# A two-layer decoder step on one core: prompt attention with half-array matmuls, a fused bias and minimum, division on GpSimd and transposes in one pass

## The chip, the core and the metric

The program runs on one core of a Trainium2 chip. A core has five engines that work side by side and signal each other by semaphores: TensorE (PE; its weight loads are shown as PEld), VectorE (DVE), ScalarE (ACT), GpSimd (POOL) and SyncE (SP), which here only issues transfers. The metric is the device time of one execution in microseconds (us), lower is better. All arithmetic is float32.

## The reference

Two layers are computed, for a prompt of 512 tokens and for 8 sampling sequences of one token each. In each layer three token mixers run on one joint input projection: a gated recurrence, gated linear attention, and sparse attention. The change lies in the third, in its part for the prompt. There are 16 heads of width 64 in 4 groups of 4 heads; a group shares keys and values. For each query three attentions are taken and added with gates:

```python
s = jnp.einsum('bqgpd,bngd->bgpqn', q, kc)
dist = (q_pos[:, None] - c_end[None, :])
p_cmp = masked_softmax(s - sl * dist, c_end[None, :] <= q_pos[:, None])   # compressed keys, 32 of them
...
p = masked_softmax(s - sl * dist, dist >= 0)                              # selected blocks
...
p = masked_softmax(s - sl * dist, mask)                                   # window of 512
...
return gates[..., 0:1] * o_cmp + gates[..., 1:2] * o_slc + gates[..., 2:3] * o_win
```

`sl` is a slope that each head has of its own. With 512 prompt tokens the second and the third see all earlier keys, so both are full causal attentions, each with keys and values of its own.

## The kernel before

The kernel is written by hand in blocks. Each block gives every engine a list of instructions, semaphores order them across engines, and a block ends when all engines have ended their lists. A layer is a chain of such blocks; the one that is changed, "the stage" below, is the prompt attention, once in each layer. The block in front of it projects and normalizes keys, values and queries (`KTR`, `VR`, `NQ`), and the one behind it is the attention of the samples, which begins by loading cache pages.

The stage walks over `NT` = 4 tiles of 128 queries (i = 0 to 3), and the keys that tile i sees are n = 128, 256, 384 or 512. Per tile it walks over the 4 groups g, and per group over 9 units: one for the compressed keys (all four heads together, 32 keys each) and 8 with one head each, 4 of the second attention and 4 of the third. That makes 144 units in each layer, 128 of them with a head. For a unit with a head:

- `scores` (L1737) on TensorE: queries by keys into a PSUM bank. A head is only 64 wide, but the query tile holds a head of an even group in its upper 64 rows and one of an odd group in its lower 64. `KTR` therefore holds zeros in the rows that belong to the other group, and the matmul takes all 128 rows.
- `biased` (L1850) on VectorE adds minus slope times distance on the way from PSUM to a buffer `SC`; `maximum` (L1863) takes the negated maximum of a row.
- `exps` (L1797) on ScalarE: exponential with the sum of each row, which takes an ACTIVATE and an ACTIVATION_READ_ACCUMULATOR.
- `scale` (L1881) and `diagonal` (L1889) on VectorE: reciprocal of the sum, and a 128x128 diagonal matrix of that reciprocal times the gate.
- `turn` (L1756) on TensorE: the probabilities are turned and divided at once by a matmul with this diagonal. A float32 matmul is two records in the trace, a transpose (L1752, L1356) is one.
- `copy` (L1810) on ScalarE brings the turned probabilities from PSUM to `PT`.
- `values` (L1773): values by probabilities, once for each group and attention, over 512 columns (four heads). Its result has 64 rows, so it uses 64 of the array's 128 columns: upper or lower half by the parity of g.

The order on each engine is written out: the score of unit u+4, the bias of u+3, the maximum of u+2 and the exponential of u are issued around the turn of u, and `values` comes three units behind. GpSimd has no work in the stage. In the block ahead of it, it sets the zeros of `KTR` (L1534).

## Time and profile before

| | us |
|---|---|
| median of 3 runs (lowest, highest) | 4429.02 (4428.1, 4430.91) |
| profiled execution, span from first to last instruction | 4429.1 |
| PE busy | 4083.6 |
| PEld busy | 3151.3 |
| DVE busy | 1352.0 |
| ACT busy | 829.6 |
| POOL busy | 140.1 |

The profiled execution agrees with the median to 0.1 us, so the span needs no correction. A busy PE is not a PE at its peak: matmuls overlap, and the busy time counts the time from a first start to a last end. How fast TensorE works is read from how far starts stand apart.

### The profile page before, as it was taken

To read this page: it belongs to the slowest core of one execution; us is meant where nothing else is said; L and a number is where in the kernel's file an instruction comes from. 1 tells how busy PE (TensorE), PEld (TensorE's weight loads), DVE (VectorE), ACT (ScalarE), POOL (GpSimd) and SP (SyncE) were. 2 spreads that over 40 slices of the span, in tenths; PEclk is the share of its full clock that TensorE was granted. 3 is DMA by queue.
4 is the path that set the end of the run, shared out by engine and by line. 5 is a ranking of instruction groups with operands and counts; after the bars stand their busy time and mean duration, and the time that the engine had idled before them with its cause. 6 is when DMAs were issued, how large, how long until landed. Compare 5 with 4: busy or idle time off the path is not lost. (4 is left out here: it accounts for less than half of the span.)

```text
span 4429.1 us, 47158 instructions
## 1 busy us (share of the span) xinstructions
PE 4083.6 (92%) x18666; PEld 3151.3 (71%) x18666; DVE 1352.0 (31%) x3077; ACT 829.6 (19%) x1710; POOL 140.1 (3%) x148
## 2 busy tenths in 40 slices
PE   7998898899899999999988988988999999999999
PEld 5757654655688887888877576546557888888888
DVE  5516433576320001000064173336763200010001
ACT  2213131254210000000032231313542000000000
POOL 0000020000110000000000000200001100000000
PEclk9999898999899999999999998988998999999999
DMA  3110442210252122212122104512004422212121
GB/s 125 60 57 25 144 152 55 79 48 1 81 176 63 56 72 76 76 67 77 38 89 78 40 23 144 171 49 105 10 1 123 134 76 76 72 42 76 67 82 52
DMA packets 222171, 336.95 MB, mean 76 GB/s; under 512 B 56614, under 2 KB 122386, under 8 KB 217210
## 3 DMA queue, kind: packets, MB, share of 16 engines
q1 hardware_dynamic: 204474, 281.90, 19.6%
q0 software_dynamic: 8064, 43.00, 2.9%
q10 hardware_dynamic: 9408, 8.98, 0.6%
q8 instruction: 150, 2.46, 0.2%
q14 instruction: 75, 0.61, 0.0%
HBM read 313.49 MB, written 37.10 MB: 79 GB/s over the span
## 5 line engine op out<-in xcount | busy, mean ns | idle before, releaser
L360 PE MATMUL pair<-hT,ring 128*128 128x260 f32 (+1 forms) x6464 | 1464.1, 388 | 75.4 <-issue 39.1
L360 PEld LDWEIGHTS pair<-hT,ring 128*128 128x128 f32 (+1 forms) x6464 | 1236.9, 192 | 288.9 <-issue 86.3
L370 PE MATMUL pair<-ring,hT 128*128 128x512 f32 (+3 forms) x960 | 385.6, 567 | 30.5 <-PEq L1263 25.6
L370 PEld LDWEIGHTS pair<-ring,hT 128*128 128x128 f32 (+1 forms) x960 | 167.0, 194 | 237.6 <-issue 237.3
L2360 PE MATMUL pair<-arena,ring 128*128 128x260 f32 x1408 | 309.1, 383 | 1.8 <-DVE arena L2386 1.8
L2360 PEld LDWEIGHTS pair<-arena,ring 128*128 128x128 f32 x1408 | 267.4, 190 | 43.5 <-DVE arena L2386 2.5
L1756 PEld LDWEIGHTS pair<-arena 128*128 128x128 f32 x1280 | 170.8, 192 | 98.6 <-DVE arena L1889 74.9
L2325 DVE TENSOR_TENSOR arena<-pair,arena 128x520 f32<-128x520 f32 x48 | 33.6, 700 | 659.4 <-PE pair L360 659.4
L1756 PE MATMUL pair<-arena 128*128 128x128 f32 x1280 | 199.1, 287 | 22.4 <-DVE arena L1889 21.6
L2386 DVE TENSOR_TENSOR arena<-pair,arena 128x520 f32<-128x520 f32 x44 | 30.8, 700 | 601.3 <-PE pair L360 601.3
L1737 PE MATMUL pair<-arena 128*128 128x128 f32 (+3 forms) x512 | 192.2, 461 | 0.0
L1850 DVE SCALAR_TENSOR_TENSOR arena<-con,pair 128x128 f32<-128x128 f32 (+3 forms) x256 | 123.6, 483 | 167.5 <-PE pair L1737 164.6
L1371 PE MATMUL pair<-arena 128*128 128x512 f32 (+1 forms) x320 | 155.4, 571 | 10.3 <-DVE arena L1485 10.3
L797 PE MATMUL pair<-hT,ring 128*128 128x260 f32 x512 | 137.2, 415 | 25.9 <-DVE ocT L1052 25.9
L1810 ACT ACTIVATE ring<-pair 128x128 f32<-128x128 f32 (+3 forms) x256 | 111.7, 436 | 254.3 <-PE pair L1756 253.1
L2310 ACT ACTIVATE arena<-pair 128x520 f32<-128x520 f32 x48 | 28.9, 603 | 668.3 <-PE pair L360 668.3
L1773 PE MATMUL pair<-ring,arena 128*64 128x512 f32 x320 | 151.0, 602 | 1.4 <-ACT ring L1810 1.4
L1797 ACT ACTIVATE arena<-arena 128x128 f32<-128x128 f32 (+3 forms) x256 | 142.5, 557 | 13.7 <-DVE arena L1863 10.9
L2375 ACT ACTIVATE arena<-pair 128x520 f32<-128x520 f32 x44 | 26.5, 603 | 606.6 <-PE pair L360 606.6
L1737 PEld LDWEIGHTS pair<-arena 128*128 128x128 f32 x512 | 79.8, 198 | 75.6 <-issue 63.7
L797 PEld LDWEIGHTS pair<-hT,ring 128*128 128x128 f32 x512 | 101.6, 208 | 44.1 <-issue 29.7
L1356 PEld LDWEIGHTS pair<-con,arena 128*128 128x128 f32 (+1 forms) x640 | 78.7, 150 | 75.8 <-issue 73.2
(351 smaller groups left out, 4414.9 us busy)
## 6 DMA issues: line engine op xcount, KB each, us to landing
ring<-in_w_in_dram SPq DMA_DIRECT2D x38, 2048.0 KB, 9.2
ring<-in_w_ffn_gate_dram SPq DMA_DIRECT2D x10, 2048.0 KB, 7.8
ring<-in_w_ffn_up_dram SPq DMA_DIRECT2D x10, 2048.0 KB, 8.1
ring<-in_w_ffn_down_dram SPq DMA_DIRECT2D x8, 2048.0 KB, 7.7
out_s_win_kv_dram<-in_cache_win_kv_dram SPq DMA_DIRECT2D x2, 8176.0 KB
arena<-in_cache_slc_kv_dram SPq DMA_DIRECT2D x86, 128.0 KB
ring<-in_cache_slc_kv_dram SPq DMA_DIRECT2D x86, 128.0 KB
arena<-in_state_gla_dram SPq DMA_DIRECT2D x16, 512.0 KB
```

Source lines behind the costliest of these rows:

```text
L360: last = pe.matmul(pair[o][0:m, half, 0:HA], lhs(k), rhs[:, k, half * HA:(half + 1) * HA], start=(k == 0), stop=(k == nk - 1))
L370: last = pe.matmul(big[0:rows, 0:w], hT[:, k, tt * P:tt * P + rows], slab[:, k, 0:w], start=(k == 0), stop=(k == KT - 1))
L797: last = pe.matmul(pair[proj_pair(key)][:, half, 0:HA], gr[0][:, k, m % 4 * P:(m % 4 + 1) * P], hT[:, k, half * HA:(half + 1) * HA], start ...
L1356: last = pe.transpose(bank[4 + kv][:, g * P:g * P + n], R2[z // 2 % 3][0:n, kv * G + g, :], ident[0:n, 0:n])
L1371: pe.matmul(dst, PH[:, kv, 2 * qt + sp2_, :], src, start=(qt == 0 and sp2_ == 0), stop=(qt == 3 and sp2_ == 1)).then_inc(sem("ct_mm"), 1)
L1737: last = pe.matmul(out[:, 0:n], NQ[:, gp * 4 + p_, i * P:(i + 1) * P], KTR[br - 1][:, g, 0:n], start=True, stop=True)
L1756: last = pe.matmul(out[:, kt * P:(kt + 1) * P], SC[u % NSC][:, kt * P:(kt + 1) * P], DG[u % 4], start=True, stop=True)
L1773: last = pe.matmul(out, VR[br - 1][:, kt, g * DH:(g + 1) * DH], PT[br][:, kt, :], start=False, stop=(br == 2 and kt == i))
L1797: act.activation(s[:, 0:n], s[:, 0:n], ACT.Exp, bias=stat[:, u % NSC, 0, 0:1], accum_out=stat[:, u % NSC, 1, 0:1]).then_inc(sem("sa_e"), 1)
L1810: act.activation(PT[br][:, 0:i + 1, p_ * P:(p_ + 1) * P], src[:, 0:(i + 1) * P].rearrange("p (k t) -> p k t", t=P), ACT.Copy).then_inc(sem ...
L1850: dve.scalar_tensor_tensor(s[:, 0:n], dist[:, 384 - i * P:384 - i * P + n], -SLOPE[4 * g + p_], src[:, 0:n], ALU.mult, ALU.add).then_inc(s ...
L2360: last = pe.matmul(pair[m][:, half, 0:HA], w[:, k, m * P:(m + 1) * P], FA[:, r + k, half * HA:(half + 1) * HA], start=(r + k == 0), stop=( ...
```

## The change

A unit now takes two groups at once, an even one (a = 0) and an odd one (a = 1), so there are 72 units in each layer, 64 of them with two heads, and the work of a unit is that of two before.

- Keys are stored without zeros. The score of a head takes 64 rows of the array, upper or lower, and the two heads of a unit follow each other in different halves, into the two banks of a PSUM pair.
- The slope is moved: the queries are divided by minus the slope when they are normalized (`qsl`), and one VectorE instruction with an accumulator (`tensor_tensor_reduce`) adds the distance, multiplies by the slope and takes the minimum of each row. It is two instructions in the program, both shown as ISA. The exponential reads the result with scale -1.
- GpSimd multiplies the probabilities in `SC` by reciprocal and gate. The diagonal matrix goes, and `turn` is now a transpose.
- `values` runs for two heads of both groups (256 columns), the two groups in turn in different column halves.
- VectorE does one of the four copies of each two units, ScalarE the other three. Of `SC` there are 5 buffers for two heads instead of 7 for one.
- The zeros of `KTR` and `KCP` are no longer set.

```diff
-                        last = pe.matmul(out[:, 0:n], NQ[:, gp * 4 + p_, i * P:(i + 1) * P],
-                                         KTR[br - 1][:, g, 0:n], start=True, stop=True)
+                        for a in range(2):
+                            hf = slice(a * DH, (a + 1) * DH)
+                            q_ = NQ[hf, gp * 4 + h + p_, i * P:(i + 1) * P]
...
+                                last = pe.matmul(out[:, a, 0:n], q_, KTR[br - 1][hf, gp, 0:n], start=True, stop=True)
...
-                            last = pe.matmul(out[:, kt * P:(kt + 1) * P], SC[u % NSC][:, kt * P:(kt + 1) * P],
-                                             DG[u % 4], start=True, stop=True)
+                            last = pe.transpose(out[:, kt * P:(kt + 1) * P], SC[v % NSC][:, a, kt * P:(kt + 1) * P], ident)
...
-                            last = pe.matmul(out, VR[br - 1][:, kt, g * DH:(g + 1) * DH], PT[br][:, kt, :],
-                                             start=False, stop=(br == 2 and kt == i))
+                    for kt in range(1 if br == 0 else i + 1):
+                        for a in range(2):
...
+                                last = pe.matmul(out[:, (p_ - 1) * P:(p_ + 1) * P], VR[br - 1][:, kt, g * DH:(g + 1) * DH],
+                                                 PT[pt_slot(v)][:, a, kt, :], start=False, stop=(kt == i),
+                                                 skip_group_check=True)
...
+                for v in range(-AHEAD_S, NU + LAG_V):
+                    if v + AHEAD_S < NU:
+                        scores(v + AHEAD_S)
+                    if 0 <= v < NU:
+                        turn(v, 0)
+                        turn(v, 1)
+                    if v >= LAG_V and (units[v - LAG_V][2] == 0 or units[v - LAG_V][3] % 2):
+                        values(v - LAG_V)
...
+            @block.gpsimd
+            def _(pool):
...
+                    pool.wait_ge(sem("sa_r"), v + 1)
...
+                            pool.tensor_scalar(s[:, a, 0:n], s[:, a, 0:n], st[:, 1, a:a + 1], GATE[:, i, k:k + 1],
+                                               ALU.mult, ALU.mult).then_inc(sem("sa_p"), 1)
...
-                        dve.scalar_tensor_tensor(s[:, 0:n], dist[:, 384 - i * P:384 - i * P + n], -SLOPE[4 * g + p_],
-                                                 src[:, 0:n], ALU.mult, ALU.add).then_inc(sem("sa_read"), 1)
+                    for a in range(2):
+                        last = dve.tensor_tensor_reduce(s[:, a, 0:n], dist[:, 384 - i * P:384 - i * P + n], src[:, a, 0:n],
+                                                        SLOPE[4 * (2 * gp + a) + p_], 3e38, ALU.add, ALU.min,
+                                                        st[:, 0, a:a + 1])
...
+                for v in range(-AHEAD_B, NU):
+                    if v + AHEAD_B < NU:
+                        biased(v + AHEAD_B)
+                    if 0 <= v + AHEAD_R < NU:
+                        inverse(v + AHEAD_R)
+                    if v >= 0 and dve_copies(v):
+                        copy(v)
```

On TensorE, at the last query tile (512 keys), the order of before is this; a row is an instruction of the program with its line, result and operands, and "x4" says how often it follows itself:

```order
L1737 MATMUL pair<-arena 128x512
L1756 MATMUL pair<-arena 128x128 x4
L1737 MATMUL pair<-arena 128x512
L1756 MATMUL pair<-arena 128x128 x4
L1773 MATMUL pair<-ring,arena 64x512 x4
L1737 MATMUL pair<-arena 128x512
```

The order now, at the same place, where L1743 is the score, L1758 the transpose and L1777 the values:

```order
L1743 MATMUL pair<-arena 128x512 x2
L1758 MATMUL pair<-con,arena 128x128 x8
L1743 MATMUL pair<-arena 128x512 x2
L1758 MATMUL pair<-con,arena 128x128 x8
L1777 MATMUL pair<-ring,arena 64x256 x8
L1743 MATMUL pair<-arena 128x512 x2
```

Two scores now stand together, eight turns (two halves of four) follow, and values come after every second unit, that is after four heads' worth of scores, with eight matmuls of 256 columns.

On VectorE, at the last query tile, the order of before for one unit of one head and the start of the next:

```order
L1850 SCALAR_TENSOR_TENSOR arena<-con,pair 128x512
L1863 TENSOR_REDUCE arena<-arena 128x1
L1889 TENSOR_SCALAR arena<-con,arena 128x128
L1881 RECIPROCAL arena<-arena 128x1
L1850 SCALAR_TENSOR_TENSOR arena<-con,pair 128x512
```

Now, for one unit of two heads and the first of the next (the order repeats with that copy after every second unit):

```order
L1889 ISA arena<-con,pair 128x512
L1889 ISA arena 128x1
L1889 ISA arena<-con,pair 128x512
L1889 ISA arena 128x1
L1908 RECIPROCAL arena<-arena 128x2
L1915 COPY ring<-pair 128x4x128
L1889 ISA arena<-con,pair 128x512
L1889 ISA arena 128x1
```

The maximum has gone into the biased operation and the diagonal is gone; one reciprocal serves two heads, and the copy from PSUM is new on this engine.

## Rows read from the trace of the kernel before

**Rows 1.** The page: span, busy time of engines (share of the span) and instructions.

```profile
span 4429.1 us, 47158 instructions
PE 4083.6 (92%) x18666; PEld 3151.3 (71%) x18666; DVE 1352.0 (31%) x3077; ACT 829.6 (19%) x1710; POOL 140.1 (3%) x148
```

**Rows 2.** Windows over the stage in the first layer; PEclk is the granted clock.

```profile
core 0: us, PE busy (x) PEld busy (x) DVE busy (x) ACT busy (x) POOL busy (x), PEclk, DMA share, GB/s
869.00:900.00 31.00, 26.66 (x129) 18.39 (x130) 23.24 (x113) 17.71 (x68) 0.00 (x0) 0.84 0.48 203
900.00:950.00 50.00, 46.27 (x230) 28.63 (x230) 37.26 (x158) 28.96 (x99) 0.00 (x0) 1.00 0.10 43
950.00:1050.00 100.00, 97.53 (x445) 56.10 (x444) 66.20 (x227) 53.72 (x150) 0.00 (x0) 1.00 0.00 1
1050.00:1160.50 110.50, 107.29 (x480) 59.61 (x480) 63.53 (x178) 51.33 (x117) 0.00 (x0) 1.00 0.00 1
```

**Rows 3.** Timeline at the stage's ends, first layer, then second (start us, us long).

```profile
869.26 1.28 ACT L1794 ACT_TABLE_LOAD   x1 [4.96 <-PEq L1525]
...
1161.40 0.59 ACT L1818 ACTIVATE ocT<-pair 64x512 f32<-64x512 f32 x1 [3.74 <-PE pair L1773]
...
3063.88 1.28 ACT L1794 ACT_TABLE_LOAD   x1 [4.96 <-PEq L1525]
...
3356.07 0.59 ACT L1818 ACTIVATE ocT<-pair 64x512 f32<-64x512 f32 x1 [3.74 <-PE pair L1773]
```

**Rows 4.** Timeline of PE around one values step, last query tile.

```profile
1101.86 1.02 PE L1737 MATMUL pair<-arena 128*128 128x512 f32 x2
1102.76 1.16 PE L1756 MATMUL pair<-arena 128*128 128x128 f32 x8
1103.85 3.65 PE L1773 MATMUL pair<-ring,arena 128*64 128x512 f32 x8
1107.43 1.12 PE L1737 MATMUL pair<-arena 128*128 128x512 f32 x2
1108.39 1.05 PE L1756 MATMUL pair<-arena 128*128 128x128 f32 x8
```

**Rows 5.** Timeline of PE in an earlier block: transposes, then matmuls.

```profile
592.83 0.60 PE L1356 MATMUL pair<-con,arena 128*128 128x128 f32 x4
593.27 1.02 PE L1371 MATMUL pair<-arena 128*128 128x512 f32 x2
594.13 0.60 PE L1356 MATMUL pair<-con,arena 128*128 128x128 f32 x4
```

**Rows 6.** Groups by shape over the first layer's stage (busy us, mean ns).

```profile
L1756 PE MATMUL pair<-arena 128*128 128x128 f32 x640 | 99.6, 287 | 11.2 <-DVE arena L1889 10.8
L1773 PE MATMUL pair<-ring,arena 128*64 128x512 f32 x160 | 75.5, 602 | 0.7 <-ACT ring L1810 0.7
L1733 PE MATMUL pair<-arena 128*128 128x32 f32 x128 | 16.5, 274 | 9.5 <-PEq L1525 9.5
L1850 DVE SCALAR_TENSOR_TENSOR arena<-con,pair 128x512 f32<-128x512 f32 x32 | 21.9, 686 | 36.2 <-PE pair L1737 36.2
L1850 DVE SCALAR_TENSOR_TENSOR arena<-con,pair 128x128 f32<-128x128 f32 x32 | 8.9, 279 | 8.2 <-PE pair L1737 8.2
L1881 DVE RECIPROCAL arena<-arena 128x1 f32<-128x1 f32 x128 | 20.0, 156 | 1.2 <-ACT arena L1797 1.2
L1797 ACT ACTIVATION_READ_ACCUMULATOR arena<-arena 128x1 f32 x128 | 24.1, 188 | 0.0
L1810 ACT ACTIVATE ring<-pair 128x512 f32<-128x512 f32 x32 | 19.1, 597 | 48.7 <-PE pair L1756 48.6
```

**Rows 7.** Groups of the whole span: a scan, a copy from PSUM, GpSimd's copies.

```profile
L704 DVE TENSOR_TENSOR_SCAN arena<-ocT,arena 128x512 f32<-128x512 f32 x16 | 19.5, 1218 | 0.0
L1485 DVE COPY arena<-pair 128x512 f32<-128x512 f32 x64 | 44.2, 691 | 97.6 <-PE pair L1356 91.1 <-PE pair L1371 6.4
L1323 POOL COPY arena<-arena 128x1024 f32<-128x1024 f32 x22 | 22.9, 1039 | 45.2 <-PE pair L1356 40.2 <-DMA arena<-in_cache_cmp_kv_dram,gather 4.9
```

**Rows 8.** Windows with a lower granted clock (columns as in rows 2).

```profile
870.00:880.00 10.00, 8.43 (x34) 6.47 (x34) 6.63 (x32) 4.67 (x18) 0.00 (x0) 0.55 0.52 211
700.00:710.00 10.00, 3.70 (x10) 2.22 (x8) 7.34 (x5) 2.76 (x4) 0.00 (x0) 0.50 0.07 30
```

More of the change, by code:

```diff
@@ L1466, in add_parts @@
                         last.then_inc(sem("ct_sum"), 1)
-                own(dve.memset(KCP, 0.0))
                 own(dve.memset(VCP, 0.0))
@@ L1509, in build @@
         NQ = sp4.take(KT, TA)
-        KTR = [sp4.take(G, T) for _ in range(2)]
+        KTR = [sp4.take(2, T) for _ in range(2)]
         VR = [sp4.take(NT, 256) for _ in range(2)]
@@ L1528, in _ @@
                 loads_of_phase(sp, 3, l)
-            @block.gpsimd
-            def _(pool):
-                for br in range(2):
-                    for a in range(2):
-                        pool.memset(KTR[br][(1 - a) * DH:(2 - a) * DH, a::2, :], 0.0)
             @block.tensor
@@ L1731, in scores, with turn @@
+                def turn(v, a):
+                    i, gp, br, p_ = units[v]
+                    pe.wait_ge(sem("sa_p"), 2 * v + a + 1)
+                    if v:
+                        pe.wait_ge(*copied(v - 1, a))
+                    out = bank[2 + a]
                     if br == 0:
                         for h in range(HPG):
[L1733 to L1738 removed]
@@ L1739, in scores @@
[L1739 to L1752 removed]
+                            last = pe.transpose(out[0:NCP, h * P:(h + 1) * P],
+                                                SC[v % NSC][:, a, h * NCP:(h + 1) * NCP], ident)
@@ L1875, in scale, with inverse @@
+                def inverse(v):
+                    i, gp, br, p_ = units[v]
+                    s, st = SC[v % NSC], stat[:, v % NSC]
+                    dve.wait_ge(sem("sa_e"), v + 1)
+                    if br == 0:
+                        s4 = heads(s[:, :, 0:P])
+                        own(dve.tensor_tensor(s4, s4, every(mcmp[:, i * NCP:(i + 1) * NCP]), ALU.mult))
+                        own(dve.tensor_reduce(st[:, 1, :].rearrange("p (a h) -> p a h", a=2), s4, AX.X, ALU.add))
                         own(dve.tensor_scalar(st[:, 1, :], st[:, 1, :], TINY, None, ALU.max))
@@ new lines, in inverse, with copy @@
+                        dve.tensor_tensor(st[:, 1, :], st[:, 1, :], gt, ALU.mult).then_inc(sem("sa_r"), 1)
+                    else:
+                        dve.reciprocal(st[:, 1, 0:2], st[:, 1, 0:2]).then_inc(sem("sa_r"), 1)
+                def copy(v):
+                    i, gp, br, p_ = units[v]
+                    dve.wait_ge(sem("sa_t"), 2 * v + 2)
+                    if v >= 4 + (br == 1):
+                        dve.wait_ge(sem("sa_pv"), value_count(v - 1 - 4 - (br == 1 and p_ < 4)))
+                    dve.tensor_copy(PT[pt_slot(v)][:, 1, 0:i + 1, P:2 * P],
+                                    bank[3][:, 0:(i + 1) * P].rearrange("p (k t) -> p k t", t=P)).then_inc(sem("sa_pd"), 1)
```

276 lines of the change are left out of this document (122 added, 154 removed).

## The prediction

> **What bounds the kernel now.** I read the page first: PE is busy 92% of the span, every other engine at most 31% [rows 1]. Then the stage alone, by its ends. It runs from the table load to the last output copy, 869.3 to 1162.0 = 292.7 us in the first layer and 3063.9 to 3356.7 = 292.8 us in the second [rows 3], together 585 of 4429 us. The stage is a block of its own, and nothing of the block behind it starts before it ends, so a us off the stage is a us off the span as long as that block does not wait for a transfer; none runs in the stage's second half (DMA share 0.00) [rows 2]. The windows show PE busy 86% at the start and 97% later, VectorE 75% falling to 57%, ScalarE 57% to 46%, GpSimd nothing [rows 2]. So TensorE bounds the stage, most clearly at the large tiles.
>
> What matters is how far its starts stand apart. A score of 512 keys is two records, and the price of such a pair and of transposes stands in an earlier block, where they alternate: from the two records of L1371 (512 columns) to the next transpose 594.13 - 593.27 = 0.86, so 0.43 each, and four transposes take 593.27 - 592.83 = 0.44, 0.11 each [rows 5]. I use 0.427 us for 512 columns in proportion to columns, 0.107 for 128. The values step confirms it: 8 records, 3.65 us less the 0.60 of the last, is 0.436 apart [rows 4, 6]. Values also cost at the edges: from the first turn record to values 1.09 us where 8 x 0.107 = 0.86 are due, from values to the next score 3.58 where 8 x 0.427 = 3.42 are due, and that score then reaches its turn in 0.96 instead of 0.86 [rows 4]. So a change of the array's form costs about 0.2 us each way.
>
> Sum for one layer before, over i (columns add up to 10 x 128 per head): scores 256 records of mean 320 columns = 68.3; turns 640 x 0.107 = 68.3 [rows 6]; values 160 x 0.427 = 68.3 [rows 6]; compressed units: 128 small scores at about 0.12 (16.5 busy us [rows 6]) = 15.7, 64 transposes = 6.9, 32 values = 13.7; 48 values steps x 0.4 = 19.2. Total 260.4. The stage takes 292.7; the 32.3 us left are its filling (at half clock, below), its drain after the last score, and waits for VectorE.
>
> **The change part by part**, one layer.
>
> *Turns.* Of 640 records 320 are left, since a transpose is one record: 34.1 instead of 68.3, saves 34.1. This price stands in rows 5.
>
> *Scores.* 256 records as before, of the same length, but alternately in the upper and the lower rows. No row shows two halves side by side. Upper bound: one after the other, 68.3. Lower bound: fully together, 34.1. Of a unit's four records the first two share a half, and so do the last two; if records start in their order and only different halves overlap, the second and third run together: 3 x 0.427 for 4. That is 51.2, and I take it. The 128 small ones likewise 15.7, 7.9, middle 11.8.
>
> *Values.* 320 records of 256 columns at 0.213 = 68.3 one after the other (half as long, twice as many). Here the halves alternate with each key tile, so a chain of 2 x (i+1) pairs overlaps except at its ends: 32 steps, (i+1) x 0.427 + 0.213 each = 34.1 + 6.8 = 41.0. Fully together: 34.1. Compressed: 13.7, 6.9, middle 10.3; their 64 transposes stay 6.9.
>
> *Changes of form.* Scores now have a form of their own (64 rows), values another (64 columns), turns the full array. Each of 72 units enters and leaves the score's form, 144 changes; each of 40 values steps adds one: 184 x 0.2 = 36.8 against 19.2, costs 17.6. The Trainium skill, TensorEngine Tiling (Array Packing), Key Properties, says that changing the tiling mode drains TensorE; the trace agrees by the 0.2 us above. Without a cost of the change of form the sum would be 17.6 us lower in each layer, and the page speaks against that.
>
> TensorE after: one by one 68.3 + 34.1 + 68.3 + 15.7 + 6.9 + 13.7 + 36.8 = 243.8; middle 51.2 + 34.1 + 41.0 + 11.8 + 6.9 + 10.3 + 36.8 = 192.1; together 34.1 x 3 + 7.9 + 6.9 + 6.9 + 36.8 = 160.8. I keep the other 32.3 as they are: filling and drain have the same steps, and values no longer hold the scores for 3.6 us, but for 1.9, which should not add waits.
>
> *VectorE.* Before, busy 190 us in the stage [rows 2]. Now 128 fused operations; the biased operation took 0.69 us at 512 columns and 0.28 at 128 [rows 6], on average 0.48, so 62; their second instructions at between nothing and ScalarE's 0.19 [rows 6], 24 at most; 64 reciprocals x 0.16 = 10 [rows 6]; 32 copies from PSUM at 0.69 [rows 7] falling to 0.29, 16; 8 compressed units with six operations of 256 columns at about 0.42 (between the 0.28 and the 0.69) and three small ones at 0.16, 24. Together 136. If the fused operation went at the pace of the scan, 1.22 us for 512 columns [rows 7], it would cost 0.53 more at 512 and 0.33 on average: 43 more, 179. Both lie below the stage's 192 + 32, so this is hidden behind TensorE; the cover ends when TensorE's share falls under it.
>
> *ScalarE.* Exponentials and their reads are unchanged in number; a quarter of the 128 copies is gone (0.60 at 512 columns [rows 6]; 32 of about 0.44 = 14), and 8 of 16 output copies. So it stays under the 152 busy us of before [rows 2]: hidden.
>
> *GpSimd.* 128 operations over 40,960 columns a layer. Its only plain rows are copies: 1.04 us for 1024 columns [rows 7], so 1.0 ns a column: 42 us. As the upper bound I double it, 84 (two scalars a column, no row for that). Hidden as throughput; as latency it stands between reciprocal and turn. The Trainium skill, GPSIMD Engine Reference, section 3.1, gives 1.8 to 2.6 cycles an element; worked out as an estimate at its 1.2 GHz that is up to 89 us, and no run here shows it.
>
> *Latency.* The tightest loop: turn, copy by VectorE, two fused operations of the next unit, reciprocal, GpSimd twice, turn two units on. At 512 keys 0.86 + 0.69 + 1.37 + 0.38 + 0.16 + 1.04 to 2.08 = 4.5 to 5.5 for two units, 2.3 to 2.8 each. TensorE needs in a middle unit there 1.28 + 0.86 + 0.96 + 0.5 = 3.6. At 128 keys the loop is about 1.2 and TensorE 1.35. It holds, barely at the first tile.
>
> *Before the stage.* The removed memsets ran on GpSimd beside the projections; one key copy less on ScalarE; VectorE loses a memset. All beside PE. Nothing.
>
> **Sum.** Saved per layer 260.4 - 192.1 = 68.3, twice 136.6: 4429.0 - 136.6 = 4292. Forecast 4292 us.
>
> **The rivals.**
>
> 1. *The halves run fully together.* For it: they use different rows, columns and banks. Against it: the order of records. 99.6 saved per layer: 4230. At a stage of 193 us VectorE with slow fused operations (179) and the loop (2.8 against 3.06) would begin to bind. The Trainium skill, TensorE: Matmul & The Clock Gate, Part 3, says that matmuls in distinct row or column groups run concurrently; its numbers are of other types of data and no run here shows it. Its rule alone would give this case or mine.
> 2. *The halves run one after the other.* The values of before, all in one half, never overlapped, but there nothing could. Then only the turns pay: 260.4 - 243.8 = 16.6 per layer, 4396.
> 3. *Another engine or the loop binds.* VectorE's fused operation at the scan's pace and GpSimd at double the copy: loop at 512 keys 5.5 + 1.06 = 6.5 for two units, 3.3 each; with 0.3 for each of four hand-overs (an estimate, the gaps of VectorE and ScalarE in rows 6 show only sums) it is 3.9 instead of 3.6, and at 128 keys 1.8 instead of 1.35. On average 0.4 x 64 = 26 per layer of my 68 go: 4344. For it: five engines in a ring with few buffers. Against: the stage of before held 97% busy with as many hand-overs.
> 4. *Slower: the granted clock falls.* It was 0.55 from 870 to 880 after PE's idle time ahead of the stage, and 0.50 from 700 to 710 with PE busy 37%, that is the 1.2 GHz level [rows 8]; in the stage it is 1.00 with PE busy 92% and more [rows 2]. After the change PE is busy less, above all at the first tiles. At 1.2 GHz records take twice as long. All of the stage at that level: 192 more per layer less 68, 4677. It decides from 68/192 = 36% of TensorE's work on: then there is no gain left. The first two tiles alone hold about 35% (1.35 + 2.1 of 9.9 us for one unit of each tile). Against: PE's share would still be 192/224 = 86%, as in the first window, most of which ran at 1.00. A case in which half of the work is slow: 192 x 0.5 - 68 = 28 per layer, 4485.
>
> **Chances.** Forecast (middle, 4250 to 4320) 0.40, together 0.22, one by one 0.17, other engine or loop 0.11, slower by the clock 0.08, gain and loss even 0.02. A measurement of this kernel tells a change from none at about 0.2%, 9 us. Slower 0.08, same 0.02, faster 0.90. Range: from 4230 with a margin of 15 for a lesser cost of form, to 4396 with a margin for waits: 4215 to 4405; left out are the clock and what lies beyond either end.
>
> **What would show it.** In the changed profile: starts of L1743 records of 512 columns: third start 0.43 after the second (one by one), at once with it (middle), four within 0.43 (together). L1758 at 0.11 apart, 320 records a layer. The 16 records of L1777 in a values step of the last tile in 1.9 us (middle), 3.4 (one by one) or 1.7 (together). L1889 at about 0.69 for 512 columns, or 1.2. L1851 on GpSimd at 0.52 for 512 columns, or 1.04. PE's idle time ahead of L1758 small; granted clock 1.00 through the stage. The stage at 224 us. What would make the prediction wrong: a PE that idles for GpSimd or VectorE at the small tiles, or a clock under 1.

## The result, and the profile after

| | median us (lowest, highest) | ratio to before [95%] |
|---|---|---|
| before, 4 runs | 4428.6 (4426.1, 4430.9) | |
| changed kernel, 4 runs | 4179.9 (4165.4, 4181.3) | 0.943 [0.942, 0.945] |
| changed kernel again, 5 runs beside 9 of before (4426.8) | 4181.2 (4173.1, 4183.0) | 0.944 [0.943, 0.945] |

The change saves 249 us, 5.6%, where 137 were forecast. The time lies 35 us below the range.

The page of the changed kernel, as rows 1:

```profile
span 4163.7 us, 45866 instructions
PE 3840.9 (92%) x18346; PEld 3005.9 (72%) x18346; DVE 1170.0 (28%) x2577; ACT 758.1 (18%) x1598; POOL 299.2 (7%) x428
```

Timeline at the stage's ends, first layer, then second (as rows 3; the first score, then the last output copy):

```profile
866.02 1.28 PE L1741 MATMUL pair<-arena 64*128 64x32 f32 x10 [9.12 <-PEq L1525]
...
1032.56 0.60 ACT L1827 ACTIVATE ocT<-pair 128x512 f32<-128x512 f32 x1 [3.51 <-PE pair L1777]
...
2927.64 1.71 PE L1741 MATMUL pair<-arena 64*128 64x32 f32 x14 [9.12 <-PEq L1525]
...
3094.16 0.60 ACT L1827 ACTIVATE ocT<-pair 128x512 f32<-128x512 f32 x1 [3.50 <-PE pair L1777]
```

The stage takes 1033.2 - 866.0 = 167.2 us in the first layer and as much in the second, instead of 292.7 and 292.8 [rows 3]: 251 us less. The gain lies there. The blocks around the stage are together 14 us shorter in this profile, which is the shortest of the kernel's runs, and 7 us shorter in the profile of the repeat, where the stage is 172.2 us. The longer stage of the repeat goes with a later rise of the clock (experiment 7).

Windows over the stage, as rows 2:

```profile
core 0: us, PE busy (x) PEld busy (x) DVE busy (x) ACT busy (x) POOL busy (x), PEclk, DMA share, GB/s
866.00:900.00 34.00, 30.05 (x197) 17.55 (x197) 19.64 (x115) 21.71 (x94) 14.85 (x34) 0.78 0.50 211
900.00:950.00 50.00, 49.92 (x355) 27.85 (x357) 33.31 (x151) 40.47 (x138) 28.58 (x53) 1.00 0.06 27
950.00:1000.00 50.00, 50.00 (x348) 27.94 (x346) 31.59 (x111) 37.54 (x103) 25.15 (x38) 1.00 0.01 1
1000.00:1033.00 33.00, 31.83 (x226) 18.27 (x220) 15.27 (x51) 21.17 (x51) 14.38 (x20) 1.00 0.00 1
```

Between 900 and the drain PE is idle for 0.1 us. VectorE is down from 190 to 100 busy us, where the prediction added up 136, and ScalarE is down from 152 to 121. GpSimd is at 83, the upper bound of the prediction (84). All three are under TensorE in each of these windows. The clock is 0.50 for the first 15 us of the stage, where before it was for 10.

Timeline of PE at the last query tile, to be set beside rows 4:

```profile
989.84 1.09 PE L1758 MATMUL pair<-con,arena 128*128 128x128 f32 x8
990.86 1.13 PE L1743 MATMUL pair<-arena 64*128 64x512 f32 x4
991.92 1.09 PE L1758 MATMUL pair<-con,arena 128*128 128x128 f32 x8
992.94 1.95 PE L1777 MATMUL pair<-ring,arena 128*64 128x256 f32 x16
994.82 1.08 PE L1741 MATMUL pair<-arena 64*128 64x32 f32 x16
```

Four score records of 512 columns, two heads, reach the next turn in 991.92 - 990.86 = 1.06 us. One head took 0.90 before [rows 4]. The record starts in the trace are 0, 0.007, 0.534 and 0.541 us into such a unit: two at a time. A view of the few ns around 991.26 shows the first two, side by side, with the other two not begun:

```profile
990.86 0.70 PE L1743 MATMUL pair<-arena 64*128 64x512 f32 x2
```

Sixteen values records reach the next score in 1.88 us, which is 16 x 0.213 / 2 = 1.71 and a change of form. Their starts also come in twos, 6 to 7 ns apart. So this is the "together" case, for scores and for values.

Groups by shape over the stage:

```profile
L1889 DVE CUSTOM_DVE_ANT_0 arena<-con,pair 128x512 f32<-128x512 f32 x32 | 20.6, 682 | 5.3 <-PE pair L1743 5.3
L1889 DVE DVE_READ_ACCUMULATOR2_ANT arena<- 128x1 f32 x128 | 10.6, 82 | 0.0
L1851 POOL TENSOR_SCALAR arena<-arena 128x512 f32<-128x512 f32 x32 | 24.2, 767 | 19.9 <-DVE arena L1908 19.7
L1851 POOL TENSOR_SCALAR arena<-arena 128x128 f32<-128x128 f32 x32 | 14.5, 463 | 11.4 <-DVE arena L1908 11.3
```

The fused operation costs what bias alone cost (0.69 [rows 6]), its read 0.08 instead of ScalarE's 0.19. GpSimd takes 0.77 us for 512 columns, between the bounds of 0.52 and 1.04, but 0.46 for 128, above both of theirs (0.13 and 0.26).

### The profile page after: what moved, and what is told of

It reads as the page before. It is cut to its first block and busy times, and to the rows that moved or that the text cites. A ratio compares the mean times of both kernels' runs of the same rounds, so it can differ in the third digit from the quotient of the medians.

```text
span 4163.7 us, 45866 instructions
## 1 busy us (share of the span) xinstructions
PE 3840.9 (92%) x18346; PEld 3005.9 (72%) x18346; DVE 1170.0 (28%) x2577; ACT 758.1 (18%) x1598; POOL 299.2 (7%) x428
## 5 line engine op out<-in xcount | busy, mean ns | idle before, releaser
L2382 PE MATMUL pair<-arena,ring 128*128 128x260 f32 x1408 | 309.1, 383 | 1.8 <-DVE arena L2408 1.8
L1851 POOL TENSOR_SCALAR arena<-arena 128x128 f32<-128x128 f32 (+3 forms) x256 | 153.8, 611 | 118.6 <-DVE arena L1908 118.0
L1889 DVE CUSTOM_DVE_ANT_0 arena<-con,pair 128x128 f32<-128x128 f32 (+3 forms) x256 | 113.7, 482 | 37.7 <-PE pair L1743 37.6
L363 PE MATMUL pair<-arena,ring 128*128 128x260 f32 x512 | 114.7, 383 | 3.1 <-DVE arena L2351 3.1
L363 PE MATMUL pair<-oaT,ring 128*128 128x260 f32 x512 | 114.8, 383 | 0.0
L363 PE MATMUL pair<-ocT,ring 128*128 128x260 f32 x512 | 114.8, 383 | 0.0
L363 PE MATMUL pair<-obT,ring 128*128 128x260 f32 x512 | 114.8, 383 | 0.0
```

Source lines behind the costliest of these rows:

```text
L363: last = pe.matmul(pair[o][0:m, half, 0:HA], lhs(k), rhs[:, k, half * HA:(half + 1) * HA], start=(k == 0), stop=(k == nk - 1))
L1851: pool.tensor_scalar(s[:, a, 0:n], s[:, a, 0:n], st[:, 1, a:a + 1], GATE[:, i, k:k + 1], ALU.mult, ALU.mult).then_inc(sem("sa_p"), 1)
L1889: last = dve.tensor_tensor_reduce(s[:, a, 0:n], dist[:, 384 - i * P:384 - i * P + n], src[:, a, 0:n], SLOPE[4 * (2 * gp + a) + p_], 3e38, ...
L2382: last = pe.matmul(pair[m][:, half, 0:HA], w[:, k, m * P:(m + 1) * P], FA[:, r + k, half * HA:(half + 1) * HA], start=(r + k == 0), stop=( ...
```

## The experiments

Sixteen runs in four series. One is the changed kernel ("after") once more; the others are after or the kernel before with the edits named. Ratios are to the kernel before on the same chip, and the differences to after take 4181 us. The kernel before has medians of 4425.5 to 4430.9 us in the four series, so a difference under 5 us between series says nothing. Where two kernels are compared stage by stage, a stage runs from TensorE's first score to the last output copy of the profile, and the time that it spends at the granted clock of 0.50 is given with it.

**1. Do the halves overlap, and when?** In the first the values loops are exchanged, in the second both scores take the upper rows.

```diff
-                    for kt in range(1 if br == 0 else i + 1):
-                        for a in range(2):
+                    for a in range(2):
+                        for kt in range(1 if br == 0 else i + 1):
```

> The changed kernel, with the values step ordered by half: all key tiles of the even group, then all of the odd group, instead of the two in turn. Same records, same work. Theory (the halves of the array work side by side only where records of different halves follow each other, and TensorE bounds the stage): a step of i+1 pairs becomes 2(i+1)-1 slots of 0.213 us, 16 steps for each tile, so 0.213 x 16 x (0+1+2+3) = 20.4 us a layer more: 4180 + 41 = 4221. Rival (the gain came from relief of VectorE, TensorE has room now): 4180, no difference. Second rival (TensorE looks further ahead than the next record): 4180 too, but with starts of the odd group's records beside those of the even group in the trace.

4203.6 us, 0.948 [0.947, 0.950]: 23 more, between the theory's 41 and nothing. Its timeline at the last tile:

```profile
1009.39 1.09 PE L1758 MATMUL pair<-con,arena 128*128 128x128 f32 x8
1010.41 2.86 PE L1777 MATMUL pair<-ring,arena 128*64 128x256 f32 x16
1013.20 1.13 PE L1743 MATMUL pair<-arena 64*128 64x512 f32 x4
```

The step takes 2.79 us instead of 1.88, at three key tiles 1.93 instead of 1.45, and at two as before, 1.02. The starts show why. With 8 + 8 records, four start alone, 0.21 to 0.27 apart; from 0.914 on two run side by side (0.914 and 0.920, 1.130 and 1.187, ...), and four come alone at the end. The trace doesn't name the half of a record, but records of one half follow each other 0.21 apart here, so the one at 0.920 is the first of the odd half. It starts together with the fifth even record, when the sixth to the eighth have not begun. With 6 + 6 records the first odd one starts with the third even one (0.484 and 0.489), with 4 + 4 with the first. So a record of the free half starts past up to three records that wait for the other half. Over 8 steps of each tile that is 8 x (0.91 + 0.48) = 11 us a layer, 22 in all, as measured. The stage agrees: 182.6 us with 30 at half pace, where the repeat of after has 172.2 with 30.

```diff
-                            hf = slice(a * DH, (a + 1) * DH)
+                            hf = slice(0, DH)
```

> The changed kernel, with both scores of a unit on the upper 64 rows (the odd group's scores are computed from the even group's queries and keys, so the result is not the reference's; the work is the same). Theory: the 256 scores of a layer follow each other at 0.427 us for 512 columns instead of two at a time, 34.1 more, the small ones 4 to 8 more, so about 40 a layer: 4180 + 80 = 4260. Rival (relief of VectorE made the gain): 4180 to 4190.

4327.7 us, 0.978 [0.975, 0.980]: 147 more, where even the theory had 80. Windows of its stage:

```profile
866.00:900.00 34.00, 31.02 (x117) 21.55 (x117) 14.21 (x78) 13.90 (x57) 8.62 (x21) 0.50 0.48 201
900.00:945.00 45.00, 45.00 (x138) 25.63 (x139) 12.96 (x74) 18.57 (x71) 12.83 (x28) 0.50 0.08 35
945.00:1000.00 55.00, 55.00 (x297) 32.86 (x295) 26.18 (x114) 31.73 (x105) 21.53 (x39) 0.93 0.01 1
```

Two things are in it. At full clock a unit of 384 keys reaches its turn in 1.49 us instead of 0.85 (records 0.32 apart after the first, none together), as the theory says. And the granted clock stays at 0.50, the 1.2 GHz level, to 949 us, although PE is busy all of the time from 880 on. The stage is 240.2 us long with 92 at half pace, where after has 167.1 with 15. As an estimate that counts half of the time at half pace as lost, the clock is (92 - 15) / 2 = 38 us a layer, and the order is the other 35, which is the theory's 34 to 42. The clock is that of the prediction's fourth rival, without the idle PE that the rival named as its cause.

**2. Halves apart.** The odd half's score goes between the two turns.

```diff
-                        scores(v + AHEAD_S)
-                    if 0 <= v < NU:
-                        turn(v, 0)
-                        turn(v, 1)
+                        scores(v + AHEAD_S, a)
+                    if 0 <= v < NU:
+                        turn(v, a)
```

(under `for a in range(2)`, and `scores` issues half a alone.)

> The changed kernel, with the odd group's score issued between the turns of the two groups: score, turn, score, turn. Theory (no overlap of scores, and 0.16 to 0.20 us for each change of the array's form): 38 to 42 a layer for the scores as in the kernel with both scores on one half, and 144 more changes of form, 23 to 29: 61 to 71 a layer, 4302 to 4322. Without a cost for the change of form: 4256 to 4264.

4465.5 us, 1.007 [1.005, 1.009]: 0.7% longer than before, with all of the change's parts in place but the order. The theory had 4302 to 4322.

```profile
900.00:1040.00 140.00, 140.00 (x385) 64.89 (x384) 36.89 (x184) 49.02 (x171) 31.36 (x62) 0.50 0.03 12
1040.00:1120.00 80.00, 80.00 (x291) 36.09 (x291) 27.49 (x101) 31.11 (x86) 20.62 (x33) 0.72 0.00 1
1120.00:1180.00 60.00, 59.32 (x308) 29.54 (x308) 24.01 (x78) 33.76 (x83) 22.80 (x32) 1.00 0.00 1
```

The clock is at 0.50 for 218 of the stage's 318 us, without a break up to 1054. By the same estimate as above the clock is 102 us a layer and the order 49, under the theory's 61 to 71. At full clock the timeline gives the price of a change of form:

```profile
1148.30 0.66 PE L1759 MATMUL pair<-con,arena 128*128 128x128 f32 x4
1148.89 1.12 PE L1743 MATMUL pair<-arena 64*128 64x512 f32 x2
1149.94 0.66 PE L1759 MATMUL pair<-con,arena 128*128 128x128 f32 x4
1150.53 1.95 PE L1778 MATMUL pair<-ring,arena 128*64 128x256 f32 x16
```

Four transposes, 0.44 us, reach the score in 0.59: 0.15. A score of 0.86 reaches the turn in 1.05: 0.19.

**3. The same score, half rows, in the kernel before.** This shows the clock without the other parts of the change.

```diff
-                        last = pe.matmul(out[:, 0:n], NQ[:, gp * 4 + p_, i * P:(i + 1) * P],
-                                         KTR[br - 1][:, g, 0:n], start=True, stop=True)
+                        last = pe.matmul(out[:, 0:n], NQ[a:a + DH, gp * 4 + p_, i * P:(i + 1) * P],
+                                         KTR[br - 1][a:a + DH, g, 0:n], start=True, stop=True)
```

> The kernel before, with its scores on 64 rows of the array (the zeros are no longer multiplied), one head at a time as before. The count and the length of TensorE's records are unchanged. By records alone: 4428. With the change of the array's form at 0.16 to 0.20 us, some 250 more changes a layer: 40 to 50 us a layer, 4508 to 4528. If unpaired half-row scores also keep the granted clock at 0.50 for a good part of the stage, as in a2 and a3: above that, 4600 to 4800.

4557.2 us, 1.029 [1.027, 1.031], 66 us a layer more for the same records on fewer rows.

```profile
880.00:970.00 90.00, 90.00 (x224) 49.18 (x223) 38.55 (x173) 28.74 (x111) 0.00 (x0) 0.50 0.16 70
970.00:990.00 20.00, 19.82 (x73) 10.62 (x73) 10.77 (x43) 8.35 (x27) 0.00 (x0) 0.83 0.00 0
990.00:1225.00 235.00, 232.44 (x956) 118.82 (x954) 136.65 (x426) 108.12 (x277) 0.00 (x0) 1.00 0.00 1
```

Before, the clock was 1.00 from 879 us on; here it is 0.50 to 977. The two stages are 356.9 and 360.3 us long with 109 and 116 at half pace, before 292.7 with 10. As an estimate by halves the clock is 49 and 53 us of the difference. Some 15 a layer are left for the changes of form, less than the 40 to 50 expected, although each costs what was expected. At full clock the step from a score to its turn takes 0.20 us more than the records alone, that from a turn to the next score 0.22. Before, with no change of form there, they took 0.11 and 0.13 more (medians), and with the diagonal on GpSimd (experiment 5) 0.01 and 0.03. So the kernel before already lost at these places a good part of what a change of form costs, by turns that waited for the diagonal.

**4. Does TensorE bind the changed stage?** The turns again take two records each.

```diff
-                            last = pe.transpose(out[:, kt * P:(kt + 1) * P], SC[v % NSC][:, a, kt * P:(kt + 1) * P], ident)
+                            last = pe.matmul(out[:, kt * P:(kt + 1) * P], SC[v % NSC][:, a, kt * P:(kt + 1) * P], ident,
+                                             start=True, stop=True)
```

> The changed kernel, with the 320 transposes of a layer done as float32 matmuls with the identity, two records each. Theory (TensorE bounds the stage throughout): 320 x 0.107 = 34.1 more a layer, 4180 + 68 = 4248. Rival (VectorE or the ring of engines now ends the waits): clearly less, 4180 to 4220.

4252.5 us, 0.960 [0.959, 0.962]: 71 more for 68 expected. TensorE's records count in full, and the rival is out.

**5. What was in the 32 us a layer that the prediction kept?** Three edits of the kernel before: the diagonal issued ahead of bias and maximum; the diagonal on GpSimd; and GpSimd dividing in place, with transposes.

```diff
                     if u >= 0:
                         scale(u)
+                    if u >= 0 and units[u][2] > 0:
+                        diagonal(u)
                     if u + AHEAD_B < NU:
```

> The kernel before, with the diagonal issued on VectorE right after the reciprocal of its unit instead of behind the bias of unit u+3 and the maximum of unit u+2. TensorE's list is unchanged. Theory (of the 32 us a layer that the prediction kept as filling and drain, 10 to 20 were turns that waited for a diagonal late on VectorE): part of them goes, 5 to 15 a layer, 4400 to 4419; since VectorE's work for a unit of 512 keys (1.86 us) is more than TensorE's (1.71), the order alone cannot free all. Rival (that time is filling, drain and a fixed cost of each step from score to turn): 4429.

4401.6 us, 0.994 [0.992, 0.996]: 27 less, 13 a layer, with TensorE's list untouched. The order of VectorE's list is what the turns waited for. The kernel before at the last tile, VectorE for one unit, then the turn that waits:

```profile
1110.41 0.69 DVE L1850 SCALAR_TENSOR_TENSOR arena<-con,pair 128x512 f32<-128x512 f32 x1 [0.40 <-PE pair L1737]
1111.02 0.68 DVE L1863 TENSOR_REDUCE arena<-arena 128x1 f32<-128x512 f32 x1
1111.61 0.34 DVE L1889 TENSOR_SCALAR arena<-con,arena 128x128 f32<-128x128 f32 x1
1111.87 0.16 DVE L1881 RECIPROCAL arena<-arena 128x1 f32<-128x1 f32 x1
1111.94 0.67 DVE L1850 SCALAR_TENSOR_TENSOR arena<-con,pair 128x512 f32<-128x512 f32 x1
...
1112.01 1.16 PE L1756 MATMUL pair<-arena 128*128 128x128 f32 x8 [0.40 <-DVE arena L1889]
```

VectorE itself waits 0.40 us for a score that only a later unit needs, then does bias and maximum, and only then the diagonal for which TensorE stands still. The starts also show that the sum of the four durations, 1.86 us, is not what a unit costs: operations overlap by some 0.08 us each, and the next bias starts 1.53 us after the first, under TensorE's 1.71. The argument of the expectation that the order alone cannot free all at 512 keys doesn't hold: there the step from score to turn falls to 0.01 us over the records, as with the diagonal on GpSimd.

```diff
+            @block.gpsimd
...
+                        pool.wait_ge(sem("sa_r"), u - u // 9)
...
+                        pool.tensor_scalar(DG[u % 4], ident, stat[:, u % NSC, 1, 0:1], GATE[:, i, k:k + 1],
+                                           ALU.mult, ALU.mult).then_inc(sem("sa_p"), 1)
```

> The kernel before, with its diagonal made by GpSimd instead of VectorE. TensorE's list is unchanged. VectorE loses 0.34 us a unit (1.86 to 1.52 at 512 keys, under TensorE's 1.71). Theory (turns waited for VectorE): 10 to 18 us a layer go, 4393 to 4409. Rival (fixed cost, filling and drain): 4429 within 5.

4393.7 us, 0.992 [0.991, 0.994]: 35 less, 17 a layer, of which the order alone brings 13. The waits of PE and of its weight loads in the stage (us, times, longest), before:

```profile
PE pair L1756 <- DVE arena L1889: 10.8, 27, 0.8
...
PEld pair L1756 <- DVE arena L1889: 37.4, 62, 1.2
```

and with the diagonal on GpSimd:

```profile
PE pair L1756 <- POOL arena L1839: 2.8, 8, 0.6
...
PEld pair L1756 <- POOL arena L1839: 7.4, 18, 0.8
```

```diff
-                            last = pe.matmul(out[:, kt * P:(kt + 1) * P], SC[u % NSC][:, kt * P:(kt + 1) * P],
-                                             DG[u % 4], start=True, stop=True)
+                            last = pe.transpose(out[:, kt * P:(kt + 1) * P], SC[u % NSC][:, kt * P:(kt + 1) * P], ident)
```

> The kernel before with one part of the change alone: GpSimd divides in place and the turns are transposes; scores, values, bias and maximum as before. TensorE loses 34.1 a layer, VectorE its diagonals. If TensorE bounds the stage and the waits for the diagonal go with it: 34 + 10 to 18 a layer, 4325 to 4341. If only the records count: 4361. Rival (VectorE's 1.52 us a unit at 512 keys is now more than TensorE's 1.28, so it binds between values steps): less than 34 a layer, 4365 to 4390.

4331.1 us, 0.978 [0.977, 0.980]: 97 less, 49 a layer, that is the transposes' 34 and 15 more, in the range of the waits. The stages of its profile are 46 us shorter each, so some 3 of the 15 lie outside of them. This one part of the change, without any half arrays, brings 39% of its gain.

**6. How much relief does VectorE need?** On the changed kernel: the division on VectorE; the minimum as an instruction of its own; both.

```diff
-                        dve.reciprocal(st[:, 1, 0:2], st[:, 1, 0:2]).then_inc(sem("sa_r"), 1)
+                        own(dve.reciprocal(st[:, 1, 0:2], st[:, 1, 0:2]))
+                        for a in range(2):
...
+                            dve.tensor_scalar(s[:, a, 0:n], s[:, a, 0:n], st[:, 1, a:a + 1], GATE[:, i, k:k + 1],
+                                              ALU.mult, ALU.mult).then_inc(sem("sa_p"), 1)
```

> The changed kernel, with the division done by VectorE instead of GpSimd. No row shows this operation at this size; the diagonal, 128 columns with two scalars, took 0.34 us on VectorE, bias 0.69 at 512. With 0.34 to 0.7 at 512 columns VectorE gets 35 to 65 us more a layer, 148 to 165 where the stage takes 167. Theory (TensorE bounds, VectorE is hidden below it): near the edge at 512 keys, where a unit costs VectorE 1.53 + 0.16 + 0.35 + 1.3 = 3.3 against TensorE's 2.9, so 5 to 20 us a layer more: 4190 to 4220. If the division on GpSimd were a bottleneck by its latency: 4170 or less.

4187.6 us, 0.945 [0.944, 0.947]: 6 more, under the theory's 10 to 40 and not clear of noise (the intervals of this and of after overlap). The stage is 174.6 us with 30 at half pace, that of the repeat of after 172.2 with 30. The operation takes 544 ns at 512 columns here, and the next one starts 461 ns after it. So the 3.3 us of the expectation, a sum of durations, is too much: by starts a unit costs VectorE 2 x 0.61 + 0.20 + 2 x 0.46 + 0.30 = 2.6 us, under TensorE's 3.0 (1.06 + 1.02 + 1.88 / 2). GpSimd's part in the gain is small.

```diff
-                        last = dve.tensor_tensor_reduce(s[:, a, 0:n], dist[:, 384 - i * P:384 - i * P + n], src[:, a, 0:n],
...
+                        own(dve.scalar_tensor_tensor(s[:, a, 0:n], dist[:, 384 - i * P:384 - i * P + n], 1.0,
+                                                     src[:, a, 0:n], ALU.mult, ALU.add))
+                        last = dve.tensor_reduce(st[:, 0, a:a + 1], s[:, a, 0:n], AX.X, ALU.min)
```

> The changed kernel, with bias and minimum as two VectorE instructions (the multiplication by the slope is left out). VectorE's busy time in the stage goes from 113 to about 164 us: at 512 keys a unit costs it 2 x (0.69 + 0.68) + 0.16 + 0.35 = 3.2 us against TensorE's 2.9, at 128 keys 1.43 against 1.35. Theory (the short TensorE list needs the relieved VectorE): 8 to 15 us a layer more, 4197 to 4211. Rival (VectorE is covered): 4181.

4215.4 us, 0.952 [0.950, 0.954]: 34 more, 17 a layer, a little over the theory's 8 to 15. The clock has no part in it: the stage is 188.2 us with 30 at half pace, against 172.2 with 30. Its first window, with scores in pairs and yet no full clock before 900:

```profile
866.00:900.00 34.00, 27.60 (x136) 15.93 (x136) 23.75 (x86) 15.63 (x63) 10.27 (x24) 0.50 0.44 185
```

By starts a unit of 512 keys costs VectorE 2 x (0.71 + 0.60) + 0.07 + 0.30 = 3.0 us here, as much as TensorE (1.06 + 1.02 + 1.88 / 2 = 3.0). The 0.71 from bias to minimum holds a wait of 0.1 us for the bias of the same head, which the order of before didn't have.

> The changed kernel, with the minimum apart (the slope left out) and the division on VectorE, so that TensorE has the changed list and VectorE all of the elementwise work. VectorE's busy time: 113 - 11 + 56 + 62 = 220 us a layer where TensorE needs 167. Theory: VectorE sets the stage, 53 us a layer more or a little over it, 4287 to 4310, and if the clock falls with a TensorE that waits, above that. Rival (TensorE sets it): 4181 to 4210.

4298.0 us, 0.971 [0.969, 0.973]: 117 more, as the theory has it. The 113 in the expectation came from windows that reach past the stage, which has 100. In its windows VectorE is the engine that doesn't rest (columns PE, PEld, DVE, ACT, POOL):

```profile
950.00:1000.00 50.00, 38.26 (x254) 20.06 (x252) 48.01 (x124) 28.89 (x80) 0.00 (x0) 0.97 0.01 1
1000.00:1090.00 90.00, 71.69 (x447) 39.05 (x448) 85.55 (x181) 52.63 (x126) 0.00 (x0) 0.94 0.00 1
```

So with VectorE's elementwise work as it was, nearly half of the change's gain would be lost: TensorE's shorter list needs the relief. The granted clock falls back to 0.50 in several short stretches of this stage; what they cost is not separated from the rest of the 117.

**7. Fewer changes of form, and the clock at the start.** First the changed kernel itself once more.

> The changed kernel once more, beside the three variants of the same chip: 4180, two stages of 167 us, and 3842 us outside the stages as in most profiles so far (3829 in the first profile of this kernel).

4181.2 us, and the profile of this run has the clock at 0.50 longer:

```profile
880.00:885.00 5.00, 5.00 (x24) 2.50 (x24) 1.36 (x11) 2.29 (x11) 2.15 (x6) 0.50 0.49 209
885.00:890.00 5.00, 5.00 (x31) 3.08 (x29) 2.55 (x11) 1.89 (x8) 1.80 (x5) 0.50 0.49 209
890.00:895.00 5.00, 5.00 (x25) 2.77 (x24) 3.07 (x20) 2.49 (x12) 2.10 (x6) 0.50 0.49 211
895.00:900.00 5.00, 5.00 (x29) 2.35 (x27) 1.51 (x12) 4.35 (x18) 2.13 (x6) 0.80 0.49 209
```

In the first profile it was 0.88 in 880 to 885 and 1.00 from 885. The stage is 172.2 instead of 167.2 us, twice, and the rest 3837 us. The time at half pace is 30 us in both stages here and 15 in both of the first profile, for the same kernel.

Then TensorE's list in steps of two units, whose scores come together:

```diff
+                for v in range(-AHEAD_S, NU + LAG_V, 2):
+                    for w in (v + AHEAD_S, v + AHEAD_S + 1):
+                        if w < NU:
+                            scores(w)
...
```

> The changed kernel, with TensorE's list grouped for two units: two units' scores, two units' turns, values. Three changes of the array's form for two units instead of five: 36 x 2 x 0.165 = 12 us a layer less, 4156, if nothing waits. Rival: the turn of the second unit now follows at once and waits for ScalarE's copy of the first out of the same bank (0.60 us and its hand-overs, where the other half's turn covers 0.43 at 512 keys), 0.3 to 0.8 us for each two units, 11 to 29 a layer: 4180 to 4215.

4195.0 us, 0.948 [0.946, 0.949]: slower than after by 14, in the rival's range. PE waits 8.7 us in 25 waits on ScalarE's copy (L1823) at the turns of one stage.

> The changed kernel, with two units' scores together, and turn, values, turn behind them where the values fall between the two turns. Three or four changes for two units instead of five: 36 x 1.5 x 0.165 = 9 us a layer less, 4162, where values cover the copy. In half of the tiles the turns still follow each other directly, with the wait of the kernel with two units: 4165 to 4195.

4175.6 us, 0.943 [0.942, 0.945]; its waits on the copy are 3.8 us in 11. Its stages are 168.2 and 168.8 us with 15 and 17 at half pace, no shorter than the 167.1 with 15 of the first profile of after. So these profiles show no gain by its list at the same clock.

Next, three full-array matmuls at the stage's beginning:

```diff
+                    if v == 2 - AHEAD_S:
+                        for w in range(3):
+                            pe.matmul(bank[5], NQ[:, w, 0:P], KTR[0][:, 0, :], start=True, stop=True)
```

> The changed kernel, with three matmuls more at the stage's beginning, 512 columns over the full array into a bank that nobody reads, while the first unit is still on VectorE. The granted clock is 0.50 from the stage's beginning to about 882 us. Theory (it rises after TensorE has worked for some time, and comes earlier with the idle time filled): 2 to 6 us a layer less, 4168 to 4176. Rival (the start of the stage is set by VectorE, or the clock doesn't come earlier): 4180 to 4186.

4175.0 us, 0.943 [0.942, 0.944]; the clock is 0.54 in 870 to 875, 0.80 in 875 to 880 and 0.86 in 880 to 885. It does come earlier, with 10 us at half pace in each stage, but the stages are 167.8 and 167.9 us, no shorter than after's best.

> The changed kernel with the list of x2 and the three matmuls of x3. x2 and x3 lay 6 us below the changed kernel each, and in x3 the granted clock rose within 10 us of the stage's beginning. If both add: 4168. If both only made the early rise of the clock likelier: 4175.

4184.3 us, 0.946 [0.945, 0.948], above both of its expectations. The intervals of after, of this and of the two before it overlap, so none is shown to be faster than the changed kernel.

## Why the prediction was wrong

The sum of one layer had a saving of 68.3 us; measured are 249 / 2 = 124. Most of the 56 between them can be put down to three of its steps:

1. **Scores and values, "middle": failed, 31 us.** The step argued from the order of a unit's four records: two on one half, then two on the other, so only the middle ones overlap. TensorE doesn't hold to it. Pairs start 7 ns apart, and the kernel with the values loops exchanged shows that a free half takes records past three that wait for the other. In a unit of four records, two on each half, no more than one such record is in the way. The together case of rival 1, 160.8 - 192.1, is this term. The rule from the Trainium skill that stood beside it, TensorE: Matmul & The Clock Gate, Part 3, that distinct row or column groups run concurrently, holds here for float32; the page names no type of data for its numbers. The same part says that matmuls start in program order, and there the starts in the kernel with the exchanged loops say otherwise (0.920 for the ninth record, 1.130 or later for three ahead of it).
2. **"I keep the other 32.3 as they are": failed, 17 us.** They were called filling, drain and waits for VectorE; of the waits it was argued only that no new ones come. With the diagonal on GpSimd and TensorE's list unchanged, 17 of them go, and 13 go by issuing the diagonal ahead of bias and maximum. So most of it was the order of VectorE's list and not its amount of work, which at 512 keys is 1.53 us a unit (by starts) against TensorE's 1.71. The 57% for VectorE in the last window [rows 2] says nothing of such a wait. The change takes the diagonal off VectorE and the maximum out of its list, so this wait had to be priced with it.
3. **Changes of form at 0.2: mis-sized, some 4 us.** In the changed kernel at full clock the medians are 0.21 from score to turn, at every number of keys, and 0.16 for the others: 72 x 0.206 + 112 x 0.163 = 33.1 instead of 36.8. The direction held, as did the rule of the Trainium skill (TensorEngine Tiling (Array Packing), Key Properties): a variant that adds changes pays 0.15 and 0.19 for them.

31.3 + 17.4 + 3.7 = 52.4 of 56. This is a ledger of terms, the second measured in the kernel before, and not a proof that they add up. The later rise of the clock went the other way: it made the stage of the repeat 5 us longer than that of the first profile. So some 4 to 9 us a layer of the gain have no measured cause; the drain, and values that hold the scores for a shorter time, were not taken apart.

What held: one-pass transposes at 0.107 us (the variant with two passes takes 71 us more, for 68 by that price); VectorE, ScalarE and GpSimd hidden; the fused operation at the price of the bias. VectorE's 136 us were too many: it is busy for 100, since the 136 add up durations that overlap, and the read was taken at up to 0.19 where it is 0.08. GpSimd's price at 512 columns was inside the bounds. At 128 columns it was not: I scaled a copy of 1024 columns down and left out a fixed part of some 0.36 us. It had next to no effect: PE waits 0.4 us for it in the stage and its weight loads 11.9, and with the division on VectorE the kernel is no faster. The Trainium skill, GPSIMD Engine Reference, 3.1, gives 1.8 to 2.6 cycles an element, as an estimate at 1.2 GHz 0.77 to 1.11 us for 512 columns and 0.19 to 0.28 for 128. The trace agrees with its lower end at 512 (0.767) and not at 128 (0.463); the sizes between them, 0.661 and 0.554, fit a fixed 0.36 us and 0.79 ns a column.

The rivals. The first, "together", had the mechanism and a chance of 0.22; its 4230 is 50 us high, 42 of them by the second and third steps above. "One by one" was priced at 4396. Tried for scores and nothing else, it is 4328 with changes of form as they are, and 4465 with the scores apart. About two thirds of what that second figure has over after is the clock, the price of rival 4. The clock was rightly on the list and wrongly bound to PE's idle time: in the three kernels with a long stretch at 0.50 PE was busy throughout, and what they have in common is that their half-row scores don't run in pairs.

## What to carry to other kernels

Half-array matmuls paid in these kernels where both halves had work within a few records of each other, with no full-array record between them. Check the order in the instruction list, and the granted clock in the windows, before counting on them. A time that is kept as "the rest" has to be split by who is waited for, above all when the change relieves that engine. Look for an operation that TensorE needs and that is issued behind others which can wait, and compare engines by how far starts stand apart, neither by shares of a stage nor by sums of durations. A cheap way to price such a wait is to issue the late operation earlier, or to move it to an idle engine, with the critical list unchanged. And before a small difference is put down to an edit, compare the time at half clock of the two profiles: one kernel had 15 us of it in one run and 30 in another.

## What the runs showed of the hardware

- Two float32 matmuls on different row halves, or on different column halves, run fully side by side: two scores of 512 columns reach the turn in 1.06 us, with both on one half in 1.91; 16 values records of 256 columns take 1.88 us, by the price of one record 3.41 if one after the other.
- TensorE starts records of a free half past up to three that wait for the other half (values loops exchanged: 4 + 4 records lose nothing, 6 + 6 take 1.93 us instead of 1.45, 8 + 8 take 2.79 instead of 1.88).
- In the three kernels whose scores take 64 rows and run singly, one of them the kernel before with nothing else changed, the granted clock was 0.50 for 82 to 187 us of a stage without a break, with PE busy all the time after the first 14 us. With paired scores it was so for 15 to 30 us at the beginning of a stage (6 to 10 where three full-array matmuls were added), with full-row scores for 10. Where VectorE bound the stage it also fell back to 0.50 later, in short stretches. Why, and why it varies from run to run of one kernel, stays open.
- A change of the array's form costs 0.15 to 0.23 us.
- VectorE's operations overlap: a bias of 512 columns is 0.69 us long, and the next operation starts 0.60 us after it.
- The fused operation with a minimum is as fast as the same pass without it (682 ns and 686 at 512 columns), and its accumulator's read takes 82 ns.
